# The ends of eight sublayers in a transformer kernel: order of the last products, the turn of the last FFN chunk, and a post-norm scale on two other engines

## The reference

```
for i in range(4):                        # mixers: diff, stick, window, diff
    hn = rms_norm(x, norm_gains[i, 0])
    m = mixer(hn)                         # attention, then o @ w_out
    x = x + rms_norm(m, norm_gains[i, 1])
    h = rms_norm(x, norm_gains[i, 2])
    f = (silu(h @ w_gate) * (h @ w_up)) @ w_down
    x = x + rms_norm(f, norm_gains[i, 3])
z = rms_norm_2(x, mix_norm) @ w_in        # dilated attention, S5, w_out
x = x + concat([attn, ssm]) @ w_out
x = x + sigmoid(rms_norm_2(x, ple_norm) @ w_ple_gate) * (p @ w_ple_proj)
```

## Time and profile before

| | us |
|---|---|
| median of 3 runs | 1469.71 (1467.35 to 1473.69) |
| the profiled execution | 1466.51 |
| its span | 1464.5 |
| PE busy in the span | 1391.3 (95%) |
| DVE busy | 1014.1 (69%) |
| ACT busy | 798.3 (55%) |
| POOL busy | 158.3 (11%) |
| one `xt_head` copy of 128x512 on ACT (L766), mean | 0.597 |
| one `xt_rest` of 128x512 on DVE (L1279), mean | 0.687 |
| one group of x turned on PE (L1976, four blocks), in the first mixer's end | 0.65 |

### The profile page before, as it was taken

How to read it: one execution, slowest core, us unless ns; L and a number is a source line. 1 busy time by engine, 2 the same in 40 slices (tenths; PEclk the granted TensorE clock), 3 DMA queues, 4 the chain that set the end, 5 groups by cost and what they waited for, 6 DMA issues and landing times.

```text
span 1464.5 us, 20490 instructions
## 1 busy us (share of the span) xinstructions
PE 1391.3 (95%) x6849; PEld 1128.3 (77%) x6849; DVE 1014.1 (69%) x1962; ACT 798.3 (55%) x1560; POOL 158.3 (11%) x303
## 2 busy tenths in 40 slices
PE   6898999998999999998999999999999999899998
PEld 5687788887888788877878888777878888777556
DVE  5987855558654855569667555589768777679876
ACT  5565654546654645456646454556655545575334
POOL 3000000000110100002000000000029992000000
PEclk9999999999999999999999999999999999999999
DMA  7443565654432656554217555544346556443132
GB/s 247 153 151 104 172 215 174 199 174 157 144 116 87 217 186 198 173 192 138 87 59 237 179 190 188 192 133 144 116 132 214 193 174 199 144 144 116 58 104 97
DMA packets 154240, 230.49 MB, mean 157 GB/s; under 512 B 7496, under 2 KB 103056, under 8 KB 154176
## 3 DMA queue, kind: packets, MB, share of 16 engines
q1 hardware_dynamic: 152176, 224.18, 46.9%
q0 software_dynamic: 2000, 5.50, 1.4%
HBM read 228.60 MB, written 1.05 MB: 157 GB/s over the span
## 4 chain that ended last, share of the span: by engine, by line
PE 86%; DVE 10%; ACT 3%; issue 1%; POOL 0%; DMA 0%; DVEq 0%; ACTq 0%; POOLq 0%
PE ps L1956 25%; PE ps L1958 24%; PE ps L1957 24%; DVE w_rest L1272 2%; PE ps L2702 1%; PE ps L2159 1%; DVE x L1333 1%; PE ps L1976 1%; PE ps L2100 1%; PE ps L2602 1%; ACT scr_a L744 1%; ACT w_head L757 1%; DVE qkv L1381 1%; DVE qkv L1379 0%; PE ps L2088 0%
## 5 line engine op out<-in xcount | busy, mean ns | idle before, releaser
L1956 PE MATMUL ps<-w_head,xt_head 128*128 128x512 f32 (+1 forms) x1344 | 531.6, 396 | 20.6 <-DVE xt_rest L1279 8.1
L1958 PE MATMUL ps<-w_head,xt_rest 128*128 128x512 f32 (+1 forms) x1344 | 518.6, 386 | 0.0
L1957 PE MATMUL ps<-w_rest,xt_head 128*128 128x512 f32 (+1 forms) x1344 | 517.7, 385 | 0.0
L1272 DVE SCALAR_TENSOR_TENSOR w_rest<-w_raw,gain_t,w_head 128x512 fp32r<-128x512 f32 (+1 forms) x600 | 415.9, 757 | 76.8 <-ACT w_head L757 76.0
L757 ACT ACTIVATE w_head<-w_raw,gain_t 128x512 fp32r<-128x512 f32 (+1 forms) x600 | 373.9, 700 | 138.7 <-PE ps L1958 121.1
L1956 PEld LDWEIGHTS ps<-w_head,xt_head 128*128 128x128 f32 x1344 | 254.3, 189 | 78.3 <-issue 14.1
L1958 PEld LDWEIGHTS ps<-w_head,xt_rest 128*128 128x128 f32 x1344 | 254.0, 189 | 51.9
L1957 PEld LDWEIGHTS ps<-w_rest,xt_head 128*128 128x128 f32 x1344 | 254.6, 189 | 46.0
L1270 DVE TENSOR_TENSOR w_rest<-w_raw,w_head 128x1024 fp32r<-128x1024 f32 x124 | 153.2, 1277 | 87.5 <-ACT w_head L757 87.5
L757 ACT ACTIVATE w_head<-w_raw 128x1024 fp32r<-128x1024 f32 x124 | 124.5, 1054 | 104.3 <-PE ps L1958 91.8
L1956 PE MATMUL ps<-w_head,ht_head 128*128 128x512 f32 x352 | 137.4, 390 | 5.6 <-DVE ht_rest L1832 5.6
(11 more groups left out here) (455 smaller groups left out, 1376.0 us busy)
## 6 DMA issues: line engine op xcount, KB each, us to landing
w_raw<-in_ffn_w_gate_dram SPq DMA_DIRECT2D x88, 512.0 KB, 4.0
w_raw<-in_ffn_w_up_dram SPq DMA_DIRECT2D x88, 512.0 KB, 4.9
w_raw<-in_ffn_w_down_dram SPq DMA_DIRECT2D x88, 512.0 KB, 4.2
w_raw<-in_a_w_in_dram SPq DMA_DIRECT2D x48, 512.0 KB, 4.7
w_raw<-in_b_w_in_dram SPq DMA_DIRECT2D x24, 512.0 KB, 4.7
w_raw<-in_w_in_dram SPq DMA_DIRECT2D x24, 512.0 KB, 4.5
w_raw<-in_a_w_out_dram SPq DMA_DIRECT2D x16, 512.0 KB, 4.2
w_raw<-in_c_w_in_dram SPq DMA_DIRECT2D x10, 512.0 KB, 4.5
```

Source lines behind the costliest of these rows:

```text
L1272: ins = dve.scalar_tensor_tensor(w_rest[:, s, w], w_raw[:, s, w], by, hd, ALU.mult, ALU.subtract)
L1956: pe.matmul(out_, hd, wh, start=first, stop=False)
L1957: pe.matmul(out_, hd, wr, start=False, stop=False)
L1958: return pe.matmul(out_, rt, wh, start=False, stop=last)
```

## The change

1. **Order on PE.** In the mixers' ends the first half's last products stand in front of the second half's (`out_tile` takes a single tile). In diff and stick fifteen matmuls of m=1 follow m=0's last, where twelve did; in window twelve as before, with one tile moved in front of `values(6)`. In the FFN a new `two_last` runs the last two chunks together.
2. **Last FFN chunk.** Its turn now lies between products of the chunk ahead, and its turned parts go to buffers of their own (`LAST_HT`, in `xt_head` and `xt_rest`). ACT copies them at once and the heads of the coming units move behind the layer end.
3. **Scale of the second half.** DVE's `posted(1, c)` goes. ACT copies the accumulator to `tok` (`taken`) and POOL multiplies it by the gain (128x512, two per end). `entered(1, c)` waits for POOL (`gained`).
4. **One step fewer** in `rsqrt_half`.
5. **DVE and ACT order** in the ends (`residual`, `close`); mixers and FFNs now share it. In an FFN's end ACT makes the head of unit u-1+RING between the last group's copy and the squares of x.
6. **Entry.** All but window's entry use `late=True`: `transposes(3)` lies amid `products(2)`. `s5_weights_turned` moves behind the entry.

```diff
...
+                    pool.wait_ge(gain_in, 16 * (i + 1))
+                    for c in range(2):
+                        pool.wait_ge(acc_taken, 2 * i + c + 1)
+                        w = cols_of(c)
+                        pool.tensor_tensor(tok[:, 1, w], tok[:, 1, w], gain[:, w], ALU.mult).then_inc(gained, 1)
+                    pool.wait_ge(gained, 2 * i + 2)
...
+            def taken(part):
+
+                m, c, bank, _ = part
+                act.activation(tok[:, m, cols_of(c)], ps[:, bank, :], ACT.Copy).then_inc(acc_taken, 1)
...
+            def close(kind, u):
+
+                these, banks = closing(kind, u)
+                squares_of(these[0:3])
+                taken(these[2])
+                squares_of(these[3:])
                 n["bank"] += banks
                 n["x"] += 4
                 entry(True, norm=False, groups=(0, 1))
+                taken(these[3])
                 head(u - 2 + RING)
                 entry(True, norm=False, groups=(2, 3))
                 head(u - 1 + RING)
...
+                act.wait_ge(hidt_ready, f + NCH)
+                act.activation(LAST_HT[0], ps[:, 6, :].rearrange("p (t c) -> p t c", t=2), ACT.Copy).then_inc(hidt_head, 1)
                 n["ffn"] += 1
-                return u
...
-                entry(True, u - 1 + RING)
...
-                step(dve.tensor_single_scalar(i_.bitcast(I32), v.bitcast(I32), 1, ALU.logical_shift_right))
-                step(dve.tensor_scalar(y.bitcast(I32), i_.bitcast(I32), -1.0, 1597463007.0, ALU.mult, ALU.add))
+                step(dve.tensor_scalar(y.bitcast(I32), v.bitcast(I32), -0.5, 1597463007.0, ALU.mult, ALU.add))
...
             def entered(m, c):
 
                 w = cols_of(c)
+                if m:
+                    dve.wait_ge(gained, 2 * n["add"] + c + 1)
                 dve.scalar_tensor_tensor(x[:, m, w], tok[:, m, w], rstd_post[:, m:m + 1], x[:, m, w], ALU.mult, ALU.add).then_inc(x_ready, 1)
...
-                step(posted(part[0, 1], at[0, 1]))
+                posted(part[0, 1], at[0, 1]).then_inc(raw_done, 1)
+                dve.wait_ge(raw_done, n["add"] + 1)
                 entered(0, 1)
-                posted(part[1, 0], at[1, 0])
                 xt_rest_of(0, True)
-                xt_rest_of(1, True)
                 mean_begun(1, at[1, 0])
                 rsqrt_half(1, at[1, 1])
                 entered(1, 0)
-                if late:
-                    rest(split - 1)
+                xt_rest_of(1, True)
+                if not narrow:
+                    rest(u - 2 + RING)
                     xt_rest_of(2, True)
-                posted(part[1, 1], at[1, 1], True)
-                dve.wait_ge(raw_done, n["add"] + 1)
                 entered(1, 1)
-                if not late:
+                if narrow:
                     xt_rest_of(2, True)
-                if not late:
-                    rest(split)
                 xt_rest_of(3, True)
-                if late:
-                    rest(split)
+                if narrow:
+                    rest(u - 2 + RING)
+                rest(u - 1 + RING)
...
-                hidt(NCH - 1)
-                rest(v + 7 + RING)
+                dve.wait_ge(hidt_head, f + NCH)
+                dve.tensor_tensor(LAST_HT[1], ps[:, 6, :].rearrange("p (t c) -> p t c", t=2), LAST_HT[0].bitcast(F32), ALU.subtract)\
+                   .then_inc(hidt_rest, 1)
...
-                for m in range(M):
-                    out_products(u + 14, 0, 4, m)
+                out_products(u + 14, 0, 4, 0)
+                pe.wait_ge(rest_done, 4 * (u + 16))
+                out_products(u + 15, 1, 4, 0)
                 tok_turned(3)
-                pe.wait_ge(rest_done, 4 * (u + 16))
-                for m in range(M):
-                    out_products(u + 15, 1, 4, m)
+                out_products(u + 14, 0, 4, 1)
+                out_tile(u + 15, 1, 4, 1)
                 pe.wait_ge(xt_rest_done, xt + 4)
-                for m in range(M):
-                    for c in range(2):
-                        out_products(u + 14 + c, c, 6, m).then_inc(unit_used if m else bank_ready, 1)
+                out_products(u + 14, 0, 6, 0).then_inc(bank_ready, 1)
+                out_products(u + 15, 1, 6, 0).then_inc(bank_ready, 1)
+                out_tile(u + 15, 1, 5, 1)
+                out_products(u + 14, 0, 6, 1).then_inc(unit_used, 1)
+                out_products(u + 15, 1, 6, 1).then_inc(unit_used, 1)
...
+                def two_last(u):
+
+                    v = u + 1
+                    pe.wait_ge(hidt_rest, f + NCH - 1)
+                    for t in range(2):
+                        pe.wait_ge(rest_done, 4 * u + 2 * t + 2)
+                        for j in range(2):
+                            down_product(u, t, 0, j)
+                    turn_hidden(NCH - 1)
+                    down_product(u, 0, 1, 0)
+                    down_product(u, 1, 1, 0)
+                    down_product(u, 0, 1, 1)
+                    pe.wait_ge(hidt_rest, f + NCH)
+                    pe.wait_ge(rest_done, 4 * v + 4)
+                    for j in range(2):
+                        down_product(v, 0, 0, j, LAST_HT)
+                        down_product(v, 1, 0, j, LAST_HT, last_=True).then_inc(bank_ready, 1)
+                    down_product(u, 1, 1, 1).then_inc(unit_used, 1)
+                    down_product(v, 0, 1, 0, LAST_HT)
+                    down_product(v, 1, 1, 0, LAST_HT, last_=True).then_inc(bank_ready, 1)
+                    down_product(v, 0, 1, 1, LAST_HT)
+                    down_product(v, 1, 1, 1, LAST_HT, last_=True).then_inc(unit_used, 1)
 
                 gate_up(u + 2, bank=4, between=lambda: turn_hidden(0))
                 down(u + 4, 0, first=True)
                 turn_hidden(1)
-                with pe.Fori(0, NCH - 2) as i:
+                with pe.Fori(0, NCH - 3) as i:
                     gate_up(u + 5, i)
                     down(u + 7, 1, i)
                     turn_hidden(2, i)
-                u += 2 + 3 * (NCH - 1)
-                down(u, NCH - 1, last_=True)
+                u += 2 + 3 * (NCH - 2)
+                gate_up(u)
+                two_last(u + 2)
...
             u = 0
             for li, kind in enumerate(layer_names):
                 m_ = MIXER[kind]
+                if li:
+                    entry(u, xs(), True, narrow=kind == "window", late=kind != "window")
+                else:
+                    entry(u, [(x_in[0], 16)] * 2 + [(x_in[1], 16)] * 2, True, between=gains_turned)
                 if li in (2, 3):
                     s5_weights_turned(2 * li - 4)
                     pe.wait_ge(wt_done, 2 * li - 2)
-                if li:
-                    entry(u, xs(), True, narrow=kind == "window")
-                else:
-                    entry(u, [(x_in[0], 16)] * 2 + [(x_in[1], 16)] * 2, True, between=gains_turned)
...
```

More of the change, by code:

```diff
@@ L1690, in window @@
                 n["o"] += 8
-                residual(u + 9, u + 9 - 1 + RING, "window")
+                residual("window", u + 9)
                 return u + 9
@@ L1770, in diff @@
                 n["o"] += 8
-                residual(u, u - 1 + RING, "diff")
+                residual("diff", u)
                 return u
@@ L1817, in stick @@
                 xt(3)
-                residual(u + 16, u + 16 - 1 + RING, "stick")
+                residual("stick", u + 16)
                 return u + 16
@@ L1926, in _ @@
                 u = ffn(u, kind == "stick")
-                residual(u, u - 1 + RING)
+                residual("ffn", u, layer_names[li + 1:li + 2] == ["window"])
             u = dilated(u)
@@ L2493, in tok_turned, with out_tile @@
                     last.then_inc(xt_ready, 1)
+                def out_tile(unit_, c, t, m):
+                    return product(ps[:, acc_bank("window", m, c), :], XT, t, m, unit_ % RING, 512 * (t % 4), 512, t == 0, t == KT - 1)
                 def out_products(unit_, c, k, m):
-                    for t in (k, k + 1):
-                        last = product(ps[:, acc_bank("window", m, c), :], XT, t, m, unit_ % RING, 512 * (t % 4), 512, t == 0, t == KT - 1)
-                    return last
+                    out_tile(unit_, c, k, m)
+                    return out_tile(unit_, c, k + 1, m)
                 for s in range(1, 5):
@@ L2541, in window @@
                 pe.wait_ge(xt_rest_done, xt + 3)
-                for m in range(M):
-                    out_products(u + 7, 0, 4, m)
+                out_products(u + 7, 0, 4, 0)
+                out_tile(u + 7, 0, 4, 1)
                 values(6)
@@ L2627, in tok_turned, with out_tile @@
                     last.then_inc(xt_ready, 1)
+                def out_tile(unit_, c, t, m):
+                    return product(ps[:, acc_bank("stick", m, c), :], XT, t, m, unit_ % RING, 512 * (t % 4), 512, t == 0, t == KT - 1)
                 def out_products(unit_, c, k, m):
-                    for t in (k, k + 1):
```

(6 more changed lines are left out.)

89 lines of the change are left out of this document (39 added, 50 removed).

## The result

The changed kernel is slower: 1479.9 us (median of 5 runs, 1477.8 to 1483.42) beside 1468.65 of the kernel before on the same chip, a ratio of 1.0088 with a 95% interval of [1.0075, 1.01]. The forecast was 1469.5, with a range from 1462 to 1475.5. The profiled execution took 1478.21 us, its span is 1476.5 us.

What follows compares the result with a forecast made beforehand. PE bounds the kernel, so only its 73 us of idling, at layer ends, can change. Layer-end terms sum to −1.0, clock adds 0.8: −0.2 on the profiled 1466.5; the median lies 3.2 higher, so 1469.5, range 1462 to 1475.5.

Steps and rivals of the forecast that it cites:

- I add up 0.85 at products(3): Layer ends: POOL's two multiplies slow DVE's sums that enter x, delaying products(3) by 0.85 us; bounds 0 and 2 × 1.1.
- Last chunk's turn: FFN ends: PE's 1.41 us wait for ht_rest, four times, 5.6 in all, is covered but for about 0.15 each.
- Mixer ends: Mixer ends: new order, shorter root and moved scale give, after contention, −0.95 twice, −0.7 in window, −1.55 in last diff.
- FFN ends, second part: FFN ends: a head ahead of the squares makes rstd_x later; net +0.2, +1.36, about 0 and +1.55 us.
- I take 0.8 in all: After PE's idle stretches in two or three FFN ends the clock halves, some 1.7 us each; 0.8 counted in all.
- B: Rival, FFN ends: norm late behind a head that may wait for a weight slot; 1475 to 1478 us; chance 0.11.
- A: Rival, layer ends: POOL's multiplies miss DVE's sums or lie in its idle time; 1463 to 1465 us; chance 0.25.
- C: Rival, FFN ends: last chunk's turn still waited for behind DVE's rest, costing 4 × 1.3; 1474.7 us; chance 0.07.
- D: Rival: transposes(3) amid products(2) and the moved s5_weights_turned remove other waits, norm not met; 1459 to 1462 us; chance 0.09.

Runs made afterwards that it cites:

- e5: Changed kernel with GpSimd's multiply cut from 512 columns to one, so the second half's gain is left out and the result differs; 1471.58 us.
- e1: Changed kernel with the second half's scale back on VectorE, without ScalarE's copies and GpSimd's multiplies; 1469.21 us.
- e11: e9 with the two heads of the FFN ends, and their rests on VectorE, put where the change puts them; 1475.07 us.
- e9: Kernel before with the last FFN chunk's turn hidden, mixers' new product order and shorter root, transposes(3) kept ahead of products(2) behind FFN ends; 1457.08 us.
- e8b: Changed kernel with s5_weights_turned and its copies back in front of the entry, in two places; 1485.1 us.
- e12: e9 with only the second half's scale moved to ScalarE and GpSimd as the change does; 1478.68 us.
- e10: e1 with, at FFN ends, the squares of x in front of ScalarE's head and the norm in front of VectorE's rest; 1466.32 us.

## Why the prediction was wrong

The profiles let each term of the sum be read by itself. For a mixer's end I take how long behind P rstd_x ends, for an FFN's end how long behind P the evacuation comes: ScalarE's first `qkv` copy, PE's first turn of an evacuated tile, VectorE's first instruction with rstd_x, PE's next product. e5 is the change without the contention. Each column is one profiled execution. In us behind P:

| | before | e5 | after |
|---|---|---|---|
| mixers' ends, rstd_x | 20.6, 20.5, 20.6, 21.4 | 18.9, 18.8, 19.4, 19.6 | 20.3, 20.4, 20.6, 21.0 |
| FFN ends, evacuation | 28.3, 18.75, 20.6, 17.2 | 29.5, 20.7, 21.6, 19.6 | 31.1, 22.2, 23.0, 21.15 |

| term | in my sum | in the profiles |
|---|---|---|
| mixers' ends without contention | −7.5 | −6.3 (e5 against before) |
| FFN: P earlier behind the mixer's rstd_x | −6.6 | −4.6 (after against before) |
| FFN: evacuation later behind P, without contention | +6.4 | +6.5 (e5 against before) |
| contention in eight ends | +6.7 | +11.6 (after against e5) |
| all between the ends, the clock above all | +0.8 | +4.7 (after against before) |
| sum | −0.2 | +12.0 |

- **The failed step: "I add up 0.85 at products(3)".** The contention between POOL's multiply and DVE costs 1.2 to 1.55 in each of the eight ends, not 0.85. The multiply lasts 1.28 (I took 1.15, near enough), the first hit cost 0.7 (I said 0.5). The second one I placed on the sum `entered(1,0)`. It fell on the root's step of one column, which stood still for 1.0 us until the multiply ended. I had counted only long instructions as exposed. I also wrote that `entered(1,0)` waits for the second multiply. It waits for the first, which was done at 148.05; the second is for `entered(1,1)`. So the 1.0 us is no wait for the product, it is contention alone. Then products(1) waited 0.69 for `w_rest` of their unit, whose rest stands behind that sum; I had no term for this. Products(3) came at P+13.8, 0.7 later than I wrote, and rstd_x 0.6 to 0.8 later in the FFN ends. By the medians e1 and e5 price the contention at 8 to 11 us. The Trainium skill ("SBUF — State Buffer", "Who interferes with whom") says that the order of issue, not the shape of the operation, decides who blocks. The 1.18 us of one column agree. The block for a whole instruction it states beside VectorE's two-port modes, and of two SBUF inputs it says that they contend; here the two hits lost 0.69 of the 0.90 us and 1.02 of the 1.16 us that were left of the multiply. I quoted that section and then priced a part of a multiply.
- **Last chunk's turn.** The waits went as forecast: 5.6 us became 0.2 (and 0.4 for `xt_rest`, the last chunk's own buffer, in the second FFN). From the mixer's rstd_x to the FFN's transposes(0) went 170.4 us instead of 172.8. P came 1.5, 1.0, 1.5 and 0.6 earlier where I wrote 1.64 each time; in the last FFN PE also waited 0.6 for `hid`.
- **Mixer ends.** Products(0) came at P+2.85, where I had P+2.5 and 0.3 of contention. Right in size.
- **FFN ends, second part.** Right in mechanism and size: e5's rstd_x ends at P+18.8 to 18.9 in three of them, where I wrote P+18.8, and e11 confirms that the moved heads delay the evacuations. In the changed kernel these came 2.8, 3.5, 2.4 and 3.9 later, 12.6 together, where my terms add to 9.7; the contention above is the difference.
- **The clock: "I take 0.8 in all".** It was 6.0 between the two profiles by the mean clocks, which are rounded, and 5.3 by the stretches. 3.4 of that lie ahead of the first changed instruction, so that part is this execution's luck and not the change. The rest, about 2, is the balance of two stretches of 3.4 and one of 1.7 at FFN ends, which came, against four of 1.7 (at 340, 954, 1046 and 1081), which went. Over all runs the lost clock differs by 0 to 4.5 us.
- **Rivals.** B had the side and nearly the size (1475 to 1478), but not for its reason: it wanted a head that waits for a weight slot, and at the last FFN's end the head starts at 1289.46, as soon as the copy in front of it is done. rstd_x came at P+20.4, at the edge of its "later than P+20.5", by the contention. That B's size nearly fits is luck. A, C and D did not happen; the ends do give 10 us (e9), about D's size, but without the late turn from which D had it.

The ledger at full clock does not add up. e9 is at 1447.7; plus 7.3 for the scale, 8.1 for the heads, 3.8 for the late turn that makes 1466.9. The changed kernel is at 1461.7. The moved s5 turn (e8b: 2.8 at full clock) and the overlap of the delays shown under e12 are on that side; how they share the 5 us was not separated.

## What to carry to other kernels

Work that is taken off VectorE and given to GpSimd on SBUF operands cost VectorE what was left of the GpSimd instruction, nearly, wherever the two met, even in a step of one column (1.0 of 1.28 us); put it where VectorE has nothing due. When casts are moved to make room for a hidden step, list what stands in front of the reduction that everyone waits for, in every queue it passes, and also what stands in front of those who use it: in e10 the reduction came 2.4 us earlier and the evacuations did not. The hidden step itself was worth 3.4 us of the 5.6 of its waits.
